# Attention of a two-layer diffusion step on one core: queries, values and heads in one pipeline, and a new order in the expert stage

## What is computed

```
h    = x * (1 + scale1) + shift1                        # modulation
proj = h @ w_in                                         # gMLP u, v | Hyena | c_q 256 | c_kv 128 | k_pe 32
q    = rms_norm(c_q) @ w_uq                             # 8 heads x (64 + 32 rotary)
k, v = rms_norm(c_kv, with 128 cached rows) @ w_ukv     # 8 heads x (64 + 64)
o    = softmax(q k^T / sqrt(96)) v                      # context reads 128 keys, latents read 384
x    = LN(alpha * x + gate1 * concat(gMLP, Hyena, o) @ w_out)
h    = x * (1 + scale2) + shift2
x    = LN(alpha * x + gate2 * HierMoE(h))               # 32 experts, top group of 4, top 2 of its 8
```

## Time and profile before

| what | value |
|---|---|
| three runs | 1299.45, 1304.18, 1312.03 us; median 1304.18 |
| profiled execution | 1298.66 us, of it 1296.9 us span |
| PE busy | 1048.1 us (81% of the span) |
| DVE, ACT, POOL busy | 542.1, 355.6, 89.8 us |
| mean granted PE clock | 0.893 |
| attention and output product, layer 0 / layer 1 | about 261 to 370 us / 848 to 963 us |
| expert stage, layer 0 / layer 1 | about 399 to 671 us / 992 to 1264 us |

### The profile page before, as it was taken

One profiled execution on the slowest core, in us unless ns is written; L12 is line 12 of the kernel. 1 busy time (PEld: TensorE's weight loads), 2 busy tenths in 40 slices (PEclk: granted clock), 3 DMA queues, 4 the chain that ended last, 5 costly groups with the idle time before them and its releaser, 6 DMA issues.

```text
span 1296.9 us, 19817 instructions
## 1 busy us (share of the span) xinstructions
PE 1048.1 (81%) x8194; PEld 618.0 (48%) x8194; DVE 542.1 (42%) x1210; ACT 355.6 (27%) x739; POOL 89.8 (7%) x97
## 2 busy tenths in 40 slices
PE   3688787888978998989854996698886998989970
PEld 2366476745445644444222756545444554435330
DVE  5530151555465142423549206544555324242346
ACT  3120003045132242423322113035222242323331
POOL 0100000010140000000007000000032000000000
PEclk8599888999977899999985998898996999998995
DMA  9857767620356779899943403010336879897941
GB/s 355 327 193 309 296 247 299 248 81 1 129 213 257 292 315 418 354 417 396 421 198 117 152 35 133 1 65 1 130 130 238 333 287 420 346 421 315 420 191 49
DMA packets 48619, 309.52 MB, mean 239 GB/s; under 512 B 6427, under 2 KB 6684, under 8 KB 15748
## 3 DMA queue, kind: packets, MB, share of 16 engines
q1 hardware_dynamic: 39516, 274.08, 52.6%
q0 software_dynamic: 7856, 31.85, 7.0%
q10 hardware_dynamic: 1144, 2.19, 0.5%
HBM read 303.11 MB, written 4.98 MB: 238 GB/s over the span
## 4 chain that ended last, share of the span: by engine, by line
PE 67%; DVE 15%; DMA 7%; ACT 6%; issue 3%; ACTq 0%; DVEq 0%; POOL 0%; SPq 0%
PE bank L913 19%; PE bank L894 8%; PE bank L856 6%; PE bank L687 5%; PE bank L1002 5%; PE bank L673 3%; DMA arena<-in_b_mod 3%; PE bank L698 2%; DMA ring<-in_w_in 2%; PE bank L763 2%; PE bank L830 2%; PE bank L775 2%; PE bank L597 1%; DVE y_lo L1890 1%; ACT y_hi L1328 1%
## 5 line engine op out<-in xcount | busy, mean ns | idle before, releaser
L894 PE MATMUL bank<-sel,h_hi 128*128 128x384 f32 x192 | 84.2, 438 | 9.4 <-DVE sel L1829 9.4
L856 PE MATMUL bank<-ring,act_t 128*128 128x512 f32 x192 | 83.3, 593 | 1.2 <-ACT act_t L1278 1.2
L614 PE MATMUL bank<-ring,arena 128*32 128x64 f32 x3072 | 60.1, 242 | 29.6 <-DMA ring<-in_w_mod 20.1
L1002 PE MATMUL bank<-y_hi,selT 128*128 128x512 f32 x144 | 61.7, 429 | 26.9 <-DVE y_lo L1890 26.6
L1306 ACT ACTIVATE arena<-bank 128x384 f32<-128x384 f32 x64 | 31.4, 491 | 173.7 <-PE bank L894 173.7
L894 PE MATMUL bank<-sel,h_lo 128*128 128x384 f32 x192 | 79.0, 411 | 0.0
L894 PEld LDWEIGHTS bank<-sel,h_hi 128*128 128x128 f32 x192 | 64.5, 336 | 30.3 <-issue 24.1
L614 PEld LDWEIGHTS bank<-ring,arena 128*32 128x32 f32 x3072 | 53.7, 124 | 42.4 <-issue 21.2
L1890 DVE SCALAR_TENSOR_TENSOR y_lo<-bank,region_v,y_hi 128x512 fp32r<-128x512 f32 x48 | 34.6, 748 | 91.7 <-ACT y_hi L1328 91.7
L687 PE MATMUL bank<-act_t,ring 128*128 128x384 f32 x192 | 66.3, 508 | 4.3 <-DMA ring<-in_w_in 4.3
L894 PEld LDWEIGHTS bank<-sel,h_lo 128*128 128x128 f32 x192 | 65.3, 340 | 0.0
(11 more groups left out here) (311 smaller groups left out, 1771.7 us busy)
## 6 DMA issues: line engine op xcount, KB each, us to landing
ring<-in_moe_gate_up SPq DMA_DIRECT2D x60, 1024.0 KB, 8.6
ring<-in_w_mod SPq DMA_DIRECT2D x48, 1024.0 KB, 9.3
region_k<-in_moe_gate_up SPq DMA_DIRECT2D x44, 1024.0 KB, 8.6
ring<-in_moe_down SPq DMA_DIRECT2D x32, 1024.0 KB, 11.2
arena<-in_moe_down SPq DMA_DIRECT2D x28, 1024.0 KB, 9.7
arena<-in_moe_gate_up SPq DMA_DIRECT2D x20, 1024.0 KB, 10.8
ring<-in_w_in SPq DMA_DIRECT2D x10, 1024.0 KB, 7.7
ring<-in_w_out SPq DMA_DIRECT2D x8, 1024.0 KB, 5.4
```

Of the source, the lines that this page charges most:

```text
L614: mm = pe.matmul(ps[MOD_BANK[g]][32 * j:32 * j + 32, c * 64:c * 64 + 64], cT[:, k, :], w[:, k, j * 64:j * 64 + 64], start=(k == 0), stop=( ...
L856: mm = pe.matmul(ps[2 * t + half][:, :], act_t[:, 2 * c + k, t * P:(t + 1) * P], w[:, k, half * 512:(half + 1) * 512], start=(c == 0 and k ...
L894: mm = pe.matmul(ps[gather_bank(o, k)][:, 0:TOK], src[:, t, k:D:K8], sel[:, t, :, :].rearrange("p v n -> p (v n)"), start=(t == 0 and i == ...
L1002: mm = pe.matmul(ps[SUM_BANKS[t]][:, :], selT[:, v, t * P:(t + 1) * P], y[:, n % 2, :], start=(v == 0 and j == 0), stop=(v == 2 and j == 1 ...
```

## The change

1. Keys: two heads per product, 128 output rows, so 4 products instead of 8. They stand first, before the wait for `yc`. The host reorders `w_ukv` so that all key columns come first.
2. Queries, values, scores and heads become one sequence. Three queries, four values and two heads' scores stand ahead; then each turn hh of the head loop issues the query of hh+3 (all from hh = 2 on in bank 7, each waiting until DVE has read the one before), the scores of hh+2, and the transposes of hh. DVE's order per turn: scale hh, maxima of hh+2, rotary of hh+3. The copies of the values go from ACT to DVE.
3. The value products of two heads are issued in turn, in column halves 0 and 64 of PE's array. `probsT` has three buffers, so PE no longer waits between transposes and products of the same head.
4. The first two of the twelve output chunks stand in the tail of the head loop, before and after the last head's transposes.
5. POOL's six affine passes wait for all of `hT` of layer 1 instead of each tile of `h`; the loads of `w_uq`, `w_ukv` and the cache stand before them now. POOL also waits for the last query before it loads a row over its input.
6. Expert stage: `place_weights` is cut in pieces and moved from the end of the oct before into the oct (for oct 0 between its gathers); `pick(1)` waits for the gathers of oct 0 alone; later picks are cut in thirds; the first part of `gate_up(o, 2)` and `gate_up(o, 4)` is issued ahead of a scatter; copies and row splits on ACT and DVE are ordered to match; the `fuse` passes are spread.

The core of the diff:

```diff
+                pool.wait_ge(s["hT"], at("hT", l))
+                for t in range(TT):
+                    affine(t, "x2")
...
             pool.wait_ge(s["v_raw"], at("v_raw", l))
+            pool.wait_ge(s["q_raw"], at("q_raw", l))
...
+            def query(hh):
+                if hh >= 2:
+                    pe.wait_ge(s["q_pe"], at("q_pe", l, max(hh, 3) if hh > 2 else 1))
                 for c in range(2):
+                    mm = pe.matmul(ps[6 if hh == 1 else 7][:, 0:TOK], wuq[:, c, hh, :], cqT[:, c, :], start=(c == 0), stop=(c == 1))
...
+            def pair_out(g):
+                pe.wait_ge(s["pT"], at("pT", l, 4 * g + 4))
+                if g > 0:
+                    pe.wait_ge(s["oT"], at("oT", l, g))
+                for i in range(4):
+                    for j in range(2):
...
+                                       tile_position=(0, 64 * j), skip_group_check=True)
...
+            for g in range(4):
+                pe.matmul(ps[g][:, :], wukv[:, P * g:P * (g + 1)], ckvT, start=True, stop=True).then_inc(s["k_raw"], 1)
+            pe.wait_ge(s["yc"], at("yc", l))
+            pe.wait_ge(s["mod_sum"], MOD_GROUPS)
+            query(0)
+            query(1)
+            value(0)
+            value(1)
+            query(2)
+            scores(0)
+            scores(1)
+            value(2)
+            value(3)
+            for hh in range(HEADS):
+                if hh + 3 < HEADS:
+                    query(hh + 3)
+                if hh + 2 < HEADS:
+                    scores(hh + 2)
+                probs_turned(hh)
+                if hh % 2 == 0 and hh > 0:
+                    pair_out(hh // 2 - 1)
+                if hh == HEADS - 2:
+                    w_out(0, 0)
+            w_out(0, 1)
+            pair_out(HEADS // 2 - 1)
...
                 gate_up(o, 0)
+                place_weights(o, 0)
                 gate_up(o, 1)
                 turns(o - 1)
                 choices(o - 1, 0)
+                place_weights(o, 1)
+                place_weights(o, 2)
                 down(o - 1, 0)
                 choices(o - 1, 1)
                 down(o - 1, 1)
+                gate_up(o, 2, over=False)
                 scatter(o - 1, 0)
                 down_over(o - 1, 0)
                 scatter(o - 1, 1)
-                gate_up(o, 2)
+                gate_up(o, 2, first=False)
...
                 ahead(5, 6, 7)
-                if o + 1 < OCTS:
-                    place_weights(o + 1)
```

and on DVE in the head loop:

```diff
             for hh in range(HEADS):
...
                 last.then_inc(s["pn"], 1)
+                if hh + 2 < HEADS:
+                    maxima(hh + 2)
+                if hh + 3 < HEADS:
+                    query(hh + 3)
```

More of the change, by code:

```diff
@@ L501, in _ @@
                 load_taps()
-                for t in range(TT):
-                    pool.wait_ge(s["h"], at("h", l, t + 1))
-                    affine(t, "x2")
             pool.wait_ge(s["h"], at("h", l))
@@ L803, in scores, with probs_turned @@
                           start=True, stop=True).then_inc(s["sc_raw"], 1)
-            scores(0)
-            scores(1)
-            for hh in range(HEADS):
-                if hh + 2 < HEADS:
-                    scores(hh + 2)
+            def probs_turned(hh):
                 pe.wait_ge(s["pn"], at("pn", l, hh + 1))
@@ new lines, in w_out @@
+            def w_out(t, c):
+                w = loaded("out", l, c).rearrange("p (k n) -> p k n", k=2)
+                if c >= 2:
+                    pe.wait_ge(s["oT"], at("oT", l, 2 * c - 2))
+                for half in range(2):
+                    for k in range(2):
+                        mm = pe.matmul(ps[2 * t + half][:, :], act_t[:, 2 * c + k, t * P:(t + 1) * P],
+                                       w[:, k, half * 512:(half + 1) * 512],
+                                       start=(c == 0 and k == 0), stop=(c == 3 and k == 1))
+                if t == TT - 1:
+                    mm.then_inc(s["chunk_done"], 1)
+                return mm
@@ L921, in copied, with gate_up @@
                 pe.wait_ge(e["copied_a"], len(CHUNKS) * l + c + 1)
-            def gate_up(o, k):
+            def gate_up(o, k, first=True, over=True):
                 c = CHUNK_AT["G", o, k]
-                pe.wait_ge(e["x_out"], K8 * (OCTS * l + o) + k + 1)
-                landed(c)
-                for v in range(VISITS):
+                if first:
+                    pe.wait_ge(e["x_out"], K8 * (OCTS * l + o) + k + 1)
+                    landed(c)
+                for v in [0, 1] * first + [2] * over:
                     if k == 0 and OCTS * l + o > 0:
@@ L1386, in _ @@
                 copy(c + 3)
-                for i in range(3):
-                    y_high(o - 1, i)
-                for n in range(4, 8):
+                y_high(o - 1, 0)
+                y_high(o - 1, 1)
+                copy(c + 4)
+                y_high(o - 1, 2)
+                for n in range(5, 8):
                     copy(c + n)
-                for i in range(3, BLOCKS):
-                    y_high(o - 1, i)
+                y_high(o - 1, 3)
+                y_high(o - 1, 4)
                 copy(c + 8)
+                y_high(o - 1, 5)
                 copy(c + 9)
@@ L1699, in maxima @@
                 dve.tensor_scalar(st[:, c:c + 3], st[:, c + 9:c + 12], -QK_SCALE, None, ALU.mult).then_inc(s["mx"], 1)
+            query(0)
+            query(1)
+            value(0)
+            value(1)
+            query(2)
             maxima(0)
+            maxima(1)
+            value(2)
+            value(3)
             for hh in range(HEADS):
-                if hh + 1 < HEADS:
-                    maxima(hh + 1)
                 c, pr = SOFT_COLS[hh % 2], probs[hh % 2]
@@ L1821, in _, with pick @@
             link(dve.tensor_reduce(place[:, :, 1, :], own_group(part), AX.X, ALU.add))
-            def pick(o):
-                for t in range(TT):
+            def pick(o, tiles=range(TT)):
+                for t in tiles:
                     dve.tensor_tensor(sel[:, t, 0:2, :], iota.unsqueeze(1).to_broadcast([P, 2, P]),
@@ L1942, in _ @@
                 choice(o - 1, 0)
+                place_weights(o)
                 copy(c + 2)
```

214 lines of the change are left out of this document (107 added, 107 removed).

## The result

The changed kernel takes 1267.75 us (median of four runs, 1261.81 to 1273.61) against 1306.31 us for the kernel before beside it; the ratio is 0.9721, 95% interval 0.9668 to 0.9775. The forecast was 1241 us, 62.7 us less than before. The profiled execution took 1264.24 us, 34.4 less than the 1298.66 of before. The direction is right and somewhat over half of the size; one stage gave almost nothing of what was put on it.

A forecast was written before the change was run, and what follows sets the result against it. It took attention as bound by a chain of waits with no engine full, the expert stage by transfers with PE close. Attention 32.6, seam 5.5 and experts 24.6 made 62.7 off 1298.66: 1236.0, or 1241 us as median; range 1222 to 1268.

The forecast's parts named there:

- The lock-step: Head loop: next query waits for DVE's rotary part, behind maxima and scores through one bank; 5.82 us a turn.
- the rival with all turns at half clock: Head loop: PE's waits halve its clock, a turn takes 8.96 us, costing 25 us over both layers; chance 0.12.
- two hidden chunks (6.9): Attention, layer 0: share of the 13.2 us saving credited to two output chunks hidden in the head loop's tail, 6.9 us.
- The forecast's own tail: Attention, layer 0: steps after query 7 is read at 304.52, ending at 321.20, with two output chunks at 3.44 us each.
- the new opening leaves no hole for the clock: Attention, layer 1: no PE idle between values and first softmax, unlike the old half-clock loop; 19.4 us less in all.
- the row of four tiles: Profile row of 12 four-column-tile products in 2.84 us, 93% of perfect fit; basis for pricing a pair at 1.55 us.
- Seam: Between the layers: with POOL moved behind hT, PE's waits of 1.50 and 3.98 us go; 5.5 us less.
- (c): Expert stage, steady transfers: three quarters of the 8.7 and 15.3 us that PE's order can win, 6.5 and 11.5.
- (b): Expert stage, end of oct 0: first freed slot reloaded earlier without place_weights there; 1.5 us less, layer 0 only.
- Term (a): Expert stage, first place_weights to next gather: shortened to 5.7 us; 3.2 and 1.9 us less in the two layers.
- The clock falls in the head loop: Rival: PE's waits in head loop turns lower its clock, costing 25 us over both layers, total 1266; chance 0.12.
- Transfers hold: Rival: in the expert stage slots, not PE's idle time, make the DMA dips; 18.0 us comes back, total 1259; chance 0.20.

The follow-up runs named there:

- rotary_first: Changed kernel with two DVE steps of the head loop exchanged: rotary part of query hh+3 before maxima of head hh+2; 1242.96 us, ratio 0.9552.
- no_tail: Changed kernel with the first two output chunks put back behind the last pair (part 4 undone); attention 97.5 and 101.0 us, whole time not given.
- old_affine: Changed kernel with POOL's six affine passes back behind each tile of h (part 5 undone); last scatter to last Hyena product 176.3 us, whole time not given.
- half_bytes: Changed kernel loading only half the columns of every expert chunk from the sixth of a layer on, all products kept; 1250.57 us, executed once.
- thin_place: Changed kernel with 3 instead of 12 products in each place_weights; 1248.73 us, executed once.
- old_place: Changed kernel with place_weights products for octs 1 to 3 back behind the last gathers of the oct before, as one lump; 1268.48 us, executed once.
- apart_only: Changed kernel with only place_weights of octs 1 to 3 taken apart, one part behind each down chunk, DVE's copy behind the second choice; 1254.27 us, ratio 0.9607.

## Why the prediction was right in part and wrong in part

**Attention: mechanism right, one attribution wrong.** The lock-step was forecast at 5.82 us a turn and is 5.93; rotary_first, which breaks it, shows that it was the bound. Turns at full clock give 96.8 less one slow turn's 1.7, and 100.2 less three of them, 95.1 both times, against 95.4 forecast. The gain is 25.9 instead of 32.6: the term that was mis-sized is the turn's time, by four turns partly at half clock, 1.7 us each; the rival with all turns at half clock (8.96 us) was too dark. Wrong is "two hidden chunks (6.9)": no_tail puts them at 0.7 and 0.8. The forecast's own tail counts both chunks in full, 3.44 each, so it hides none. What was booked there is the pairs: counted from start to start of PE's instructions in layer 0, the heads' value products took 13.3 us before and take 6.8, the keys 7.0 and 3.6; these 9.9 are most of the gain, and of the overlap PE's idle time shows 2.4. In layer 1 the forecast held that the new opening leaves no hole for the clock; the holes came in the turns themselves, 2.1 us each, and half-clock time went from 12.8 to 10.2 only.

**Pairs.** 1.73 against 1.55 priced in the same kind of row; by pace, from a pair's first instruction to the one behind the pair, 1.66 (316.28 - 314.62). One head's value products took 13.3/8 = 1.67 before, so a pair costs what one head did. By the rule of the Trainium skill, "TensorE: Matmul & The Clock Gate", Part 3, on packing small matmuls, the estimate would have been 1.96: the trace is nearer to the row of four tiles.

**Seam.** 5.5 forecast; old_affine puts it at 176.3 - 169.9 = 6.4. The stretch fell by 8.9. Counted as in the second table it holds 109.4 to 109.5 us of work at full clock in all three kernels; idle time is 49.9 us before, 49.6 in old_affine and 45.6 in the changed kernel, half-clock time 39.0, 34.4 and 29.6. So the waits gave 4.3 of the 8.9 and the clock, which the forecast left out, 4.7; and the 2.5 beyond old_affine are clock as well, which one execution of each does not tie to any edit. "SBUF — State Buffer" of the Trainium skill, "Who interferes with whom", has DVE and GpSimd share one port pair under an exclusive lock, and a DVE instruction with two inputs in SBUF, as these passes are, contend with a GpSimd instruction that reads it; 3.27 us beside POOL and 1.22 without it agree.

**Expert stage: the step that failed.** It is "(c) ... Removing the waits before scatters leaves PE about level with the DMA ... so I take three quarters", 18.0 us. The steady transfers became 2.0 and 1.2 us longer instead. The step took PE's 173.8 and 177.8 busy us for what would remain once the waits were gone; they became 183.4 and 185.9. Counted the same way, idle time in that stretch fell by 7.5 and 6.8, but work rose by 3.7 in both layers and half-clock time by 11.7 and 8.7. The waits did go (10 us at scatters, 5 at stage copies, layer 0). What the step left out, by the second table for the whole stage:
1. New waits. Moving `place_weights` out of the oct's end uncovers SiLU in octs 1 to 3, +5.6 us; (b) saw it for the end of oct 0 alone. Landings add 4.6 and 1.4. Idle time fell by 4.1 and 5.2 only.
2. The clock. `place_weights` took its dip along into the oct, and the SiLU wait made a new one; half-clock time rose by 1.1 and 8.2, which costs half. Each of these dips stands behind one of the two, but the total lies within the 21.3 to 40.2 us of other executions of the same order, so how much of the 8.2 the order makes is not shown.
3. Work rose by 1.0 and 0.8.
The sum is -4.1 + 0.6 + 1.0 = -2.5 in layer 0 and -5.2 + 4.1 + 0.8 = -0.3 in layer 1; measured -2.4 and -0.3. Term (a) came as forecast: from the first gather to the end of oct 1's gathers 398.62 to 454.28 took 55.7 us and 390.04 to 442.35 takes 52.3, in layer 1 53.9 and 51.9, so 3.4 and 2.0 us less against 3.2 and 1.9; it was then lost to 1 and 2.

**The rivals.** "The clock falls in the head loop" (1266) is nearest to the 1267.75, by luck: it put 25 us on the loop, which cost 6.8, and left the expert stage its 24.6. "Transfers hold" (1259) had the right stage and half of the cause. half_bytes takes all landings away and wins only 2.2 and 8.5 us, so they did not hold the stage; yet thin_place and old_place show that they stand directly behind: once PE gains more than a few us without releasing the slots more evenly, they take the rest.

## What to carry to other kernels

When PE and the transfers both fill a stage, count the stage as work at full clock, idle time and half-clock time, and ask of each piece of work that is moved which wait it covered: here `place_weights` covered SiLU, and a lump of one-column products took a clock dip with it wherever it went. Where one accumulator bank goes round between PE and another engine, that engine should free it before it does anything else: exchanging two steps on DVE was worth 17 us of attention. A few small products are better set one at a time between dense ones than in a lump.

## What the hardware did that was not expected

Behind the first gathers, half-clock stretches in the expert stages lasted 3.4 us each, some 6.8 or 10.2, one 17.1, and cost PE half of that. In the ten stages of the changed kernel's order each came behind 1.4 to 3.1 us of idle time or, with no idle time ahead of it, behind the lump of `place_weights` (454.51 to 456.69 us in the changed kernel, 128x1 products, with turns and a choice ahead of it from 453.06), in which the profile shows PE as busy. The same wait of 1.41 us before the first chunk of oct 2 was followed by a dip in apart_only (granted 0.66 between 509.5 and 513.0 us) and by none in the changed kernel, so between runs of nearly the same order the clock can differ by some us per stage; what decides it stays open.
